# High and low parts of the projected rows in one tensor, and one 128-partition load for a query, a key's high part and compression rows

## The chip, the cores and the metric

One core of one Trainium2 chip runs the kernel. The metric is the device time of one execution in microseconds. Three runs of the kernel before gave 3173.43, 3173.92 and 3177.03 us, with a median of 3173.92 us.

## What is computed

One transformer layer over 2048 tokens of width 1024, in float32. Cut to what matters:

```python
h = rmsnorm(x, g_mix_pre)
z = h @ w_in                                   # queries, keys, values of all mixers, split by columns
o_a = nsa_mixer(...)                           # 6 heads: compressed + selected + window attention
o_b = dilated_mixer(...)                       # 3 pairs (window, dilation) x 4 heads
o_c = banded_attention(cq, ck, cv, 127, sinks) # 6 heads, window 128
x = x + rmsnorm(concatenate([o_a, o_b, o_c]) @ w_out, g_mix_post)
x = x + rmsnorm(conv_glu_ffn(rmsnorm(x, g_ffn_pre)), g_ffn_post)
```

The compression in `nsa_mixer` runs a small two-layer network over windows of 32 keys (and values), 16 apart.

## The kernel before

The program has four parts that follow one another, each a block in which the five engines run programs of their own with semaphores set by hand: `project` (to about 684 us), `compress` (to 723), `attend` (to about 1616) and `mix_ffn`. A block begins when all engines have left the one before.

Products in float32 are made of two roundings: a value is split in a high part (rounded) and a low part (the rest). `project` computes z transposed, one row of 2048 tokens for each of 33 x 128 columns of z, and stores the high parts in the DRAM tensor `z_hi` and the low ones in `z_lo` (lines 380 and 381). The rows that the compression needs go to `z_pair`, as (key or value, parity of the token, row, 1024 tokens).

`load_windows` (line 76) fetches compression rows for m = 0 (keys) and m = 1 (values): for each of two groups, the even tokens to partitions 0 to 63 and the odd ones to partitions 64 to 127, four loads of 256 KB for each m. SP issues them at the end of `project`'s program, with the 2 MB of first-layer weights (`load_first`, line 86) behind each m. In `compress` SP then loads the small weights, the queries of the first two attention units (lines 1227, 1228), two bias tables, and the first half of what the second key needs (`keys_in`, lines 1236, 1237). The block ends on SP with a wait for `units_in`, that is for the queries and the bias tables.

`attend` works through 36 units in a fixed order: six times a k unit (compressed keys) and two b units, then six c units, then six pairs of a w unit and an s unit. A unit has 16 steps, one for 128 tokens of queries. For a step PE makes scores with two products (lines 1907, 1908): the stationary operand is a query of 128 partitions, 64 rows of its high part over 64 rows of its low part; it meets `k_hi`, the key's high part twice (partitions 0 to 63 and 64 to 127), and `k_lo`, the low part over zeroes. So hi x hi, lo x hi and hi x lo are summed. DVE adds the bias and takes maxima (line 2108), ACT exponentiates (2022), PE turns the weights and multiplies them by values (1919, 1952). PE issues scores up to five steps ahead; its order is fixed, so a missing query or key holds up the turns and value products behind it, too.

A query and a key have two buffers each. A unit's query is two loads of 512 KB (`load_q`, lines 1681, 1682), a key three: the high part twice and the low part (`load_k`, lines 1693, 1694). SP issues them when the scores of the last unit that used the buffer are done (`sp.wait_ge(scored, through(u))`), then waits for `biased` and loads the bias table (`near`, line 1704), waits for `summed` and loads the values (line 1697), then waits for the output and stores it. The k units have no key load, since their keys stay on the chip. The three heads of a group share a key in the c, w and s units. PE waits for a query with its count of 32 for each turn of the buffer, and for a key with 48 (lines 1873 to 1879).

All of these transfers are issued on SP's hardware queue. There is one group of 16 DMA engines for the core, and a transfer's semaphore rises by 16 when all of it has landed.

Of the kernel before, what the change touches and what calls it, by code (L numbers as in the profile page):

```python
# [7 lines left out]
F32 = mybir.dt.float32  # L8
# [6 lines left out]
P = 128  # L15
T = 2048
# [59 lines left out]
def load_windows(eng, z_pair, x_raw, x_in, m):  # L76

    for g in range(2):
        for odd in range(2):
            eng.dma_start(x_raw[odd * HD:(odd + 1) * HD, m, g, :],  # L80
                          z_pair[m, odd, g * HD:(g + 1) * HD, :]).then_inc(x_in[m], 16)


def load_first(eng, w1_copy, w1_raw, w1_in, m):
# [1074 lines left out]


def compress(nc, z_pair, w1_copy, b1_t, w2, overlap, x_raw, w_raw, w_hi, poss, x_in, w_in, pos_in, last_out, keys_in, kc_hi, kc_lo, vk, idt,
             z_hi, z_lo, bias_b, cmp_bias, low, near):

    U = T // 2
    NW = NC + 3
# [1 line left out]
    with ExitStack() as ctx:  # L1167
# [48 lines left out]
        @blk.sync  # L1216
        def _(sp):
            load_first(sp, w1_copy, w_raw, w_in, 1)
            sp.dma_start(b1s[:], b1_t).then_inc(small_in, 16)
            for dup in range(2):  # L1220
                sp.dma_start(kw2[:, :, dup, :], w2[0].rearrange("(m p) n -> p m n", p=P)).then_inc(small_in, 16)
            sp.dma_start(vw2[:], w2[1].rearrange("(m p) n -> p m n", p=P)).then_inc(small_in, 16)

            first = attention_units()[:3]
            for s, unit in enumerate(first[:2]):
                rows = slice(unit.q_row, unit.q_row + HD)
                sp.dma_start(low[0:HD, s, :].bitcast(F32), z_hi[rows, :]).then_inc(units_in, 16)
                sp.dma_start(low[HD:P, s, :].bitcast(F32), z_lo[rows, :]).then_inc(units_in, 16)
            sp.dma_start(near[:, 0, 0:CW], cmp_bias[0]).then_inc(units_in, 16)
            sp.dma_start(near[:, 1, 0:2 * P], bias_b[0]).then_inc(units_in, 16)  # L1230
            rows = slice(first[2].k_row, first[2].k_row + HD)
            sp.wait_ge(zeroed, 3)
            for g in range(G):
                sp.dma_start(vk[:, g, HD + 1:], overlap).then_inc(over_in, 16)
            for half in range(2):
                sp.dma_start(low[half * HD:(half + 1) * HD, 2, :].bitcast(F32), z_hi[rows, :]).then_inc(keys_in, 16)
            sp.dma_start(low[0:HD, 3, :].bitcast(F32), z_lo[rows, :]).then_inc(keys_in, 16)
            sp.wait_ge(over_in, 16 * G)
            sp.wait_ge(last_out, 4 * 16)
            sp.wait_ge(units_in, 16 * 6)  # L1240

        @blk.gpsimd
        def _(pool):
# [55 lines left out]
        @blk.scalar  # L1299
        def _(act):  # L1300
            def upper(m):
                act.wait_ge(x_in[m], 64)
                for g in range(G):
                    act.activation(inside(x_hi, m, g), every_eighth(x_raw[:, m, g, :]), ACT.Copy).then_inc(xhi_done, 1)
                act.wait_ge(w_in[m], 16)
                for c in range(1 - m, 4):
                    act.activation(w_hi[:, m, quarter(c)], w_raw[:, m, quarter(c)], ACT.Copy).then_inc(whi_done, 1)

            act.wait_ge(pos_in, 32)
            for m in range(2):  # L1310
                for g in range(G):
                    act.activation(behind(x_hi, m, g), every_eighth(poss[:]), ACT.Copy).then_inc(poshi_done, 1)
            upper(0)
            upper(1)
            for m in range(2):
                for half in range(2):
                    act.wait_ge(hb_done, 2 * m + half + 1)
                    act.activation(h1[:, m, half, :].rearrange("p (g c) -> p g c", g=G),
                                   hid[:, 2 * m + half, 0:G * NW].rearrange("p (g c) -> p g c", g=G)[:, :, 0:NC],
                                   ACT.Gelu_apprx_tanh, bias=hb[:, m, half:half + 1]).then_inc(gelu_done, 1)  # L1320
            act.wait_ge(zeroed, 3)
            act.wait_ge(kc_done, 1)
            act.activation(kc_hi[:, :, 0:NC], kc_ps[:, 0:G * NC].rearrange("p (g c) -> p g c", g=G),
                           ACT.Copy).then_inc(khi_done, 1)
# [116 lines left out]
NARROW = 5 * P  # L1441


def attend(nc, idt, z_hi, z_lo, v_heads, gates, bias_b, bias_c, bias_s, bias_w, own_block, sinks, cmp_bias, pick_bias,
           kc_hi, kc_lo, vk, sel_t, parts, near_parts, o_heads, o_mid, q2, k_hi, k_lo, near, w_small, qm, vs,
           wo_copy, wo_moved, w_rows, w_in, first_o, o_last, keys_in):

# [122 lines left out]
    with ExitStack() as ctx:  # L1570
# [96 lines left out]
            v_count.append(v_seen[owner])  # L1667
        k_count, k_seen = [], [0, 0]
        for n, s in enumerate(kv_at.slot):
            k_seen[s] += 48 if n != 1 else 0  # L1670
            k_count.append(k_seen[s])
        out_count, out_seen = [], [0, 0]
        for n, s in enumerate(out_at.slot):
# [3 lines left out]
        @blk.sync  # L1677
        def _(sp):
            def load_q(n, u):
                rows, s = slice(units[u].q_row, units[u].q_row + HD), q_at.slot[n]  # L1680
                sp.dma_start(q2[0:HD, s, :].bitcast(F32), z_hi[rows, :]).then_inc(q_in[s], 16)
                sp.dma_start(q2[HD:P, s, :].bitcast(F32), z_lo[rows, :]).then_inc(q_in[s], 16)

            def load_qm(u):
                rows = slice(units[u].q_row, units[u].q_row + HD)
                sp.wait_ge(sel_out[units[u].h // R], 64)
                sp.dma_start(qm[0:HD, :].bitcast(F32), z_hi[rows, :]).then_inc(qm_in, 16)
                sp.dma_start(qm[HD:HD + NS, :].bitcast(F32), sel_t[units[u].h // R]).then_inc(qm_in, 16)

            def load_k(n, u):  # L1690
                rows, s = slice(units[u].k_row, units[u].k_row + HD), kv_at.slot[n]
                for half in range(2):
                    sp.dma_start(k_hi[s][half * HD:(half + 1) * HD, :].bitcast(F32), z_hi[rows, :]).then_inc(k_in[s], 16)
                sp.dma_start(k_lo[s][0:HD, :].bitcast(F32), z_lo[rows, :]).then_inc(k_in[s], 16)

            def load_v(n, u):
                sp.dma_start(vs[:, kv_at.slot[n]], v_heads[units[u].v_head]).then_inc(v_in[kv_at.slot[n]], 16)
# [168 lines left out]
        def _(pe):  # L1866
            def scores(n, only):
# [2 lines left out]
                ks = kv_at.slot[kv_at.of_unit[u]] if unit.kind != "k" else None  # L1870
                if t == 0 and only == 0:
                    if q_at.turn[q_at.of_unit[u]]:
                        pe.wait_ge(q_in[qs], 32 * q_at.turn[q_at.of_unit[u]])
                    if u == 1:
                        pe.wait_ge(zeroed, 1)
                    if unit.kind != "k" and kv_at.of_unit[u] == 1:
                        pe.wait_ge(keys_in, 48)
                    elif unit.kind != "k":
                        pe.wait_ge(k_in[ks], k_count[kv_at.of_unit[u]])
                    if unit.chosen:  # L1880
                        pe.wait_ge(qm_in, 32 * qm_at.of_unit[u] + 32)
                        pe.wait_ge(own_done, 1)
# [1349 lines left out]
def layer(nc, x, g_mix_pre, g_mix_post, g_ffn_pre, g_ffn_post, w_z, w_v, pos_t, w1, b1_t, w2, sinks, w_out, w_ffn,  # L3232
# [1 line left out]
    def scratch(name, shape, dt=F32):  # L3234
        return nc.dram_tensor(name, shape, dt, kind="Internal").ap()

    z_hi, z_lo = scratch("z_hi", [NZ * P, T]), scratch("z_lo", [NZ * P, T])
    v_heads, gates = scratch("v_heads", [2 * NV - 2, P, NT, HD + 1]), scratch("gates", [P, NT, 3 * NH_A])
    sel_t = scratch("sel_t", [G, NS, T])
    z_pair = scratch("z_pair", [2, 2, P, T // 2])  # L3240
# [6 lines left out]
    with ExitStack() as keep:  # L3247
# [13 lines left out]
        with ExitStack() as rows:  # L3261
            ops_f, ops = twin(nc, rows, "ops", [P, 10, T])
            poss = rows.enter_context(nc.sbuf_tensor("poss", [P, CMP // 2 + 8], F32))
            x_raw = ops[:, 2:4, :].bitcast(F32).rearrange("p m (g u) -> p m g u", g=G)
            w1_hi = ops[:, 0:8, :].rearrange("p (m a) (b n) -> p m a b n", m=2, n=HID)[:, :, 0:2].rearrange("p m a b n -> p m (a b) n")
            w1_raw = ops[:, 6:10, :].bitcast(F32).rearrange("p (m a) (b n) -> p m (a b) n", m=2, n=HID)
            project(nc, x, g_mix_pre, idt, ident, w_z, w_v, pos_t, z_hi, z_lo, z_pair, v_heads, gates, w1, w1_copy, w_out, wo_copy, wo_moved,
                    ops_f, ops, low, kc_f[:].rearrange("p a g n -> p (a g n)"), near[:].rearrange("p s n -> p (s n)"),
                    x_raw, w1_raw, poss, x2_in, w1_in, pos_in, last_out)
            compress(nc, z_pair, w1_copy, b1_t, w2, overlap, x_raw, w1_raw, w1_hi, poss, x2_in, w1_in, pos_in, last_out, keys_in,  # L3270
                     kc_hi, kc_lo, vk, idt, z_hi, z_lo, bias_b, cmp_bias, low, near)
        w_in = keep.enter_context(nc.semaphore("w_out_in"))
        k0_hi_f, k0_hi = twin(nc, keep, "k0_hi", [P, T])
        k0_lo_f, k0_lo = twin(nc, keep, "k0_lo", [P, T])
# [3 lines left out]
        with ExitStack() as mid:  # L3278
# [2 lines left out]
            first_o = low[:, 0, :].bitcast(F32).rearrange("p (k n) -> p k n", n=D)  # L3281
            narrow = w_small[:].rearrange("p s n -> p (s n)")
            w_rows += [narrow[:, a * D:(a + 1) * D] for a in range(3)] + [near[:].rearrange("p s n -> p (s n)")[:, 0:D]]
            attend(nc, idt, z_hi, z_lo, v_heads, gates, bias_b, bias_c, bias_s, bias_w, own_block, sinks, cmp_bias, pick,
                   kc_hi, kc_lo, vk, sel_t, parts, near_parts, o_heads, o_mid, low[:, 0:2, :],
                   (k0_hi[:], low[:, 2, :]), (k0_lo[:], low[:, 3, :]), near, w_small, qm, vs, wo_copy, wo_moved, w_rows, w_in, first_o, o_last, keys_in)
            mix_ffn(nc, idt, o_heads, o_mid, first_o, o_last, w_rows, w_in, x, g_mix_post, g_ffn_pre, g_ffn_post, x1, h2_rest, g_up,
# [61 lines left out]
```

## Time and profile before

| | |
|---|---|
| median of three runs | 3173.92 us |
| span of the profiled execution | 3174.1 us, of which PE is busy 3066.0 |
| granted clock of PE, mean | 0.991 of full speed |
| DMA, mean over the span | 134 GB/s |
| `project` | 0 to 684 us |
| `compress` | 684 to 723 us |
| k and b units, c units | 723 to 1104 us |
| w and s units | 1104 to 1616 us |

The page's first part gives the busy time of each engine. A view of stretches gives the same for a part of the span, with the granted clock and the mean busy share of the 16 DMA engines (which can come out slightly over 1) and what they moved. Issues of transfers are rows of SP's queue, and their time is that of the issue; "to landing" is the time from issue to the rise of the semaphore.

### The profile page before, as it was taken

Reading aid. Unit: us, or ns where it says so; the run is one execution under the profiler, and the core shown is the slowest. Engines: PE = TensorE matmul, PEld = TensorE weight load, DVE = VectorE, ACT = ScalarE, POOL = GpSimd, SP = SyncE. Lnnn points to the kernel's source line nnn. Section 1 sums busy time; section 2 is a strip of 40 time slices with the busy share of each in tenths; the row PEclk is TensorE's granted clock in tenths of the full one; section 3 lists DMA queues with packets and bytes.
Section 4 is the critical chain, followed back from the end, with each engine's and each line's share of the span. In section 5 each row is a group of like instructions: output and inputs, shape, how many; then the busy total and the mean of one; then the engine's idle time right before and its main releaser. Section 6 shows DMA issues by size and latency. Waiting matters only on the chain. (4 is left out here: it accounts for less than half of the span.)

```text
span 3174.1 us, 44910 instructions
## 1 busy us (share of the span) xinstructions
PE 3066.0 (97%) x16138; PEld 2501.5 (79%) x16138; DVE 2058.5 (65%) x3930; ACT 1472.0 (46%) x2657; POOL 1211.7 (38%) x845
## 2 busy tenths in 40 slices
PE   8999999998998999999989989999999999999998
PEld 8888888887776776666668878888888788888887
DVE  5565566556767987777744587777645577777443
ACT  5332533236666866665633444444434344444332
POOL 2444254310000024442110098888210698885010
PEclk9999999998999999999999999999999999999999
DMA  4465555378778743332234522222565222223553
GB/s 141 161 186 149 169 162 174 114 209 195 183 187 215 175 114 73 96 99 50 84 93 132 162 99 80 87 80 80 175 200 201 102 85 80 93 80 110 182 199 106
DMA packets 262540, 425.58 MB, mean 134 GB/s; under 512 B 126801, under 2 KB 162897, under 8 KB 250321
## 3 DMA queue, kind: packets, MB, share of 16 engines
q1 hardware_dynamic: 252752, 385.28, 41.4%
q0 software_dynamic: 9568, 37.43, 3.7%
q8 instruction: 131, 2.15, 0.3%
q14 instruction: 89, 0.72, 0.1%
HBM read 304.19 MB, written 126.84 MB: 136 GB/s over the span
## 5 line engine op out<-in xcount | busy, mean ns | idle before, releaser
L1080 PE MATMUL z_banks<-ops,z_area 128*128 128x512 f32 x1720 | 434.1, 391 | 3.2 <-DVE z_area L834 3.2
L3153 PE MATMUL f_banks<-f_wt 128*128 128x512 f32 x1776 | 406.1, 389 | 0.0
L3153 PEld LDWEIGHTS f_banks<-f_wt 128*128 128x128 f32 x1776 | 333.3, 188 | 69.2
L1080 PEld LDWEIGHTS z_banks<-ops,z_area 128*128 128x128 f32 x1720 | 323.0, 188 | 70.4 <-DVE z_area L834 3.6
L2540 POOL TENSOR_TENSOR f_wt<-f_wt_f,f_wt 128x1024 fp32r<-128x1024 f32 x132 | 320.2, 2449 | 60.3 <-ACT f_wt L2668 59.4
L2022 ACT ACTIVATE w_small<-w_small,a_stats 128x128 f32<-128x128 f32 (+3 forms) x510 | 257.3, 517 | 110.7 <-DVE a_stats L2108 82.6
L3124 PE MATMUL f_banks<-low,f_wt 128*128 128x512 f32 x704 | 275.3, 391 | 0.0
L2108 DVE CUSTOM_DVE_ANT_0 w_small<-a_s_ps,near 128x128 f32<-128x128 f32 (+2 forms) x456 | 166.2, 392 | 110.1 <-PE a_s_ps L1908 86.8
L2949 DVE SCALAR_TENSOR_TENSOR near<-w_small,vk,near 128x1024 f32<-128x1024 f32 x88 | 232.3, 2640 | 1.7
L3124 PE MATMUL f_banks<-f_oo,f_wt 128*128 128x512 f32 x704 | 218.0, 391 | 3.2 <-issue 3.0
L1952 PE MATMUL a_ot_ps<-a_turned_w,vs 128*64 128x256 f32 (+3 forms) x1452 | 220.9, 427 | 0.0
L1919 PE MATMUL a_t_ps<-idt,w_small 128*128 128x128 f32 x1092 | 214.7, 283 | 5.1 <-DVE a_turned_w L2011 2.6
L2011 ACT ACTIVATE a_turned_w<-a_t_ps 128x512 f32<-128x512 f32 (+3 forms) x255 | 137.2, 545 | 150.5 <-PE a_t_ps L1919 150.4
L2949 DVE SCALAR_TENSOR_TENSOR w_small<-w_small,vk 128x1024 f32<-128x1024 f32 x88 | 158.7, 1803 | 62.3 <-ACT w_small L2728 62.3
L2960 DVE TENSOR_TENSOR f_wt<-f_wt_f,f_wt 128x512 fp32r<-128x512 f32 x88 | 60.8, 690 | 205.6 <-ACT f_wt L2741 205.3
L3089 PE MATMUL f_banks<-f_wt,f_oo 128*128 128x512 f32 x768 | 179.3, 392 | 1.4 <-DVE f_wt L2503 1.4
L1952 PEld LDWEIGHTS a_ot_ps<-a_turned_w,vs 128*64 128x64 f32 x1452 | 105.9, 136 | 93.4 <-issue 76.0
L2733 ACT ACTIVATE near<-near 128x1024 f32<-128x1024 f32 x44 | 46.7, 1062 | 267.1 <-DVE near L2949 267.1
L1080 PE MATMUL z_banks<-low,z_area 128*128 128x512 f32 x560 | 168.3, 390 | 2.1 <-DVE z_st_lo L892 2.0
L2011 DVE COPY a_turned_w<-a_t_ps 128x512 f32<-128x512 f32 (+3 forms) x255 | 158.8, 624 | 17.5 <-PE a_t_ps L1919 15.6
L2738 ACT ACTIVATE f_wt<-f_wt_f 128x1024 fp32r<-128x1024 f32 x74 | 78.3, 1058 | 194.7 <-DMA f_wt_f<-in_w_ffn 194.6
L3089 PEld LDWEIGHTS f_banks<-f_wt,f_oo 128*128 128x128 f32 x768 | 142.7, 188 | 31.6 <-DVE f_wt L2503 2.7
(305 smaller groups left out, 7120.4 us busy)
## 6 DMA issues: line engine op xcount, KB each, us to landing
f_wt_f<-in_w_ffn SPq DMA_DIRECT2D x74, 512.0 KB, 4.1
z_area_f<-in_w_z SPq DMA_DIRECT2D x54, 512.0 KB, 5.1
low<-z_hi SPq DMA_DIRECT2D x48, 512.0 KB, 7.9
f_raw_f<-in_w_ffn SPq DMA_DIRECT2D x22, 1024.0 KB, 4.8
f_wt_f<-in_w_ffn SPq DMA_DIRECT2D x22, 1024.0 KB, 5.3
g_up<-near SPq DMA_DIRECT2D x44, 512.0 KB, 2.6
f_wt_f<-g_up SPq DMA_DIRECT2D x88, 256.0 KB, 4.4
low<-z_lo SPq DMA_DIRECT2D x39, 512.0 KB, 8.6
```

The source lines that it names most:

```text
L1080: last = pe.matmul(banks[:, bank, :], w[:, c * P:(c + 1) * P], rows[:, c * 512:(c + 1) * 512], start=(first and c == 0 and q == 0), stop=( ...
L1919: ins = pe.transpose(t_ps[:, b % TB, i, :], weights(n)[:, x * P:(x + 1) * P], idt[:])
L1952: ins = pe.matmul(ot_ps[lines, at:at + count * P], values, rows, start=(x == mine[0]), stop=(x == mine[-1]), skip_group_check=True)
L2011: ins = eng.activation(out, src, ACT.Copy) if e == 0 else eng.tensor_copy(out, src)
L2022: act.activation(weights(n), weights(n), ACT.Exp, bias=negm[:, n % 32:n % 32 + 1], scale=-1.0, accum_out=total).then_inc(weighed, 1)
L2108: dve.tensor_tensor_reduce(weights(n)[:, a:z], s_ps[:, c % SB, 0:z - a], table[:, at + a:at + z], -0.125, floor, ALU.add, ALU.min, low).th ...
L2540: pool.tensor_tensor(a_lo(n, first, count), src, a_hi(n, first, count).bitcast(F32), ALU.subtract)\
L2738: act.activation(hi, raw, ACT.Copy).then_inc(wdh_done, 1)
L2949: dve.scalar_tensor_tensor(out=acc[b], in0=u[:, b, i:HALF + i], scalar=cw[:, b, i, j:j + 1], in1=acc[b], op0=ALU.mult, op1=ALU.add).then_i ...
L3089: last = pe.matmul(mix[:, k, n * 512:(n + 1) * 512], oo[:, k, part, c, :], w_part(w, c)[:, n, :], start=(c == 0 and i == 0), stop=(c == DC ...
L3124: last = pe.matmul(banks[:, 4 * (n % 2) + bank, :], w[:, c * P:(c + 1) * P], rows[:, c * 512:(c + 1) * 512], start=(first and c == 0 and x ...
L3153: last = pe.matmul(banks[:, 2 * t + n, :], g[:, tok], w[:, n, :], start=(d == 0 and x == 0), stop=(d == NF - 1 and x == 2))
```

## The change

`z_hi` and `z_lo` become two halves of one DRAM tensor `z_parts` of shape (2, 33 x 128, 2048); `project` writes them as before. A unit's query is fetched by one load whose source is (2 parts, 64 rows, 2048), and a key's high part by one load whose source is the same 64 rows with a step of 0 over a leading count of 2. Compression rows come with source (2 parities, 64 rows, 1024). The destination of each has 128 partitions. The low part of a key stays a load of 64 partitions. The counts in the waits follow. Nothing is moved in the order of any engine.

```diff
 def load_windows(eng, z_pair, x_raw, x_in, m):
 
     for g in range(2):
-        for odd in range(2):
-            eng.dma_start(x_raw[odd * HD:(odd + 1) * HD, m, g, :],
-                          z_pair[m, odd, g * HD:(g + 1) * HD, :]).then_inc(x_in[m], 16)
+        eng.dma_start(x_raw[:, m, g, :], z_pair[m, :, g * HD:(g + 1) * HD, :]).then_inc(x_in[m], 16)
+
+
+def both_parts(z_parts, row):
+
+    return z_parts[:, row:row + HD, :]
+
+
+def upper_twice(z_parts, row):
+
+    return z_parts[0, row:row + HD, :].unsqueeze(0).to_broadcast([2, HD, T])
...
             for s, unit in enumerate(first[:2]):
-                rows = slice(unit.q_row, unit.q_row + HD)
-                sp.dma_start(low[0:HD, s, :].bitcast(F32), z_hi[rows, :]).then_inc(units_in, 16)
-                sp.dma_start(low[HD:P, s, :].bitcast(F32), z_lo[rows, :]).then_inc(units_in, 16)
+                sp.dma_start(low[:, s, :].bitcast(F32), both_parts(z_parts, unit.q_row)).then_inc(units_in, 16)
...
-            for half in range(2):
-                sp.dma_start(low[half * HD:(half + 1) * HD, 2, :].bitcast(F32), z_hi[rows, :]).then_inc(keys_in, 16)
-            sp.dma_start(low[0:HD, 3, :].bitcast(F32), z_lo[rows, :]).then_inc(keys_in, 16)
+            sp.dma_start(low[:, 2, :].bitcast(F32), upper_twice(z_parts, first[2].k_row)).then_inc(keys_in, 16)
+            sp.dma_start(low[0:HD, 3, :].bitcast(F32), z_parts[1, rows, :]).then_inc(keys_in, 16)
...
-            sp.wait_ge(units_in, 16 * 6)
+            sp.wait_ge(units_in, 16 * 4)
...
-                act.wait_ge(x_in[m], 64)
+                act.wait_ge(x_in[m], 32)
...
-            k_seen[s] += 48 if n != 1 else 0
+            k_seen[s] += 32 if n != 1 else 0
...
             def load_q(n, u):
-                rows, s = slice(units[u].q_row, units[u].q_row + HD), q_at.slot[n]
-                sp.dma_start(q2[0:HD, s, :].bitcast(F32), z_hi[rows, :]).then_inc(q_in[s], 16)
-                sp.dma_start(q2[HD:P, s, :].bitcast(F32), z_lo[rows, :]).then_inc(q_in[s], 16)
+                s = q_at.slot[n]
+                sp.dma_start(q2[:, s, :].bitcast(F32), both_parts(z_parts, units[u].q_row)).then_inc(q_in[s], 16)
 
             def load_qm(u):
                 rows = slice(units[u].q_row, units[u].q_row + HD)
                 sp.wait_ge(sel_out[units[u].h // R], 64)
-                sp.dma_start(qm[0:HD, :].bitcast(F32), z_hi[rows, :]).then_inc(qm_in, 16)
+                sp.dma_start(qm[0:HD, :].bitcast(F32), z_parts[0, rows, :]).then_inc(qm_in, 16)
                 sp.dma_start(qm[HD:HD + NS, :].bitcast(F32), sel_t[units[u].h // R]).then_inc(qm_in, 16)
 
             def load_k(n, u):
                 rows, s = slice(units[u].k_row, units[u].k_row + HD), kv_at.slot[n]
-                for half in range(2):
-                    sp.dma_start(k_hi[s][half * HD:(half + 1) * HD, :].bitcast(F32), z_hi[rows, :]).then_inc(k_in[s], 16)
-                sp.dma_start(k_lo[s][0:HD, :].bitcast(F32), z_lo[rows, :]).then_inc(k_in[s], 16)
+                sp.dma_start(k_hi[s].bitcast(F32), upper_twice(z_parts, units[u].k_row)).then_inc(k_in[s], 16)
+                sp.dma_start(k_lo[s][0:HD, :].bitcast(F32), z_parts[1, rows, :]).then_inc(k_in[s], 16)
...
-                        pe.wait_ge(q_in[qs], 32 * q_at.turn[q_at.of_unit[u]])
+                        pe.wait_ge(q_in[qs], 16 * q_at.turn[q_at.of_unit[u]])
...
-                        pe.wait_ge(keys_in, 48)
+                        pe.wait_ge(keys_in, 32)
...
-    z_hi, z_lo = scratch("z_hi", [NZ * P, T]), scratch("z_lo", [NZ * P, T])
+    z_parts = scratch("z_parts", [2, NZ * P, T])
+    z_hi, z_lo = z_parts[0], z_parts[1]
```

## Rows read from the trace of the kernel before

**Rows 1.** Busy time of the engines, from the page's first part

```profile
PE 3066.0 (97%) x16138; PEld 2501.5 (79%) x16138; DVE 2058.5 (65%) x3930; ACT 1472.0 (46%) x2657; POOL 1211.7 (38%) x845
```

**Rows 2.** Stretches: start:end, length, busy by engine, PE clock, DMA share, GB/s

```profile
675.00:723.00 48.00, 41.39 (x303) 38.30 (x301) 21.92 (x24) 20.44 (x25) 6.11 (x8) 1.00 1.05 248
...
723.00:739.00 16.00, 13.77 (x54) 11.01 (x54) 8.38 (x40) 8.36 (x20) 1.75 (x1) 0.51 0.74 181
...
723.00:1129.00 406.00, 372.75 (x2764) 300.10 (x2765) 307.09 (x1367) 285.58 (x915) 10.14 (x15) 0.96 0.81 193
...
1129.00:1600.00 471.00, 452.14 (x2908) 323.59 (x2907) 355.74 (x1250) 289.29 (x585) 151.09 (x199) 1.00 0.31 79
```

**Rows 3.** PE's waits: line, releaser, us in total, times, longest

```profile
PE a_s_ps L1907 <- DVE a_stats L2108: 19.5, 27, 2.3
```

**Rows 4.** Line 2108, 700 to 1110 us: what ended its engine's idle time

```profile
  DMA near<-in_bias_b: 9.1, 4
...
  DMA near<-in_cmp_bias: 1.5, 1
```

**Rows 5.** Timeline of PE: start, us, line, operation

```profile
720.62 1.10 PE L1295 MATMUL c_vc_ps<-c_vw,c_h 128*127 128x64 f32 x8
...
1103.21 0.30 PE L1907 MATMUL a_s_ps<-k_hi,low 128*128 128x128 f32 x1
```

**Rows 6.** Timeline of SP's queue around the compression

```profile
675.23 2.42 SPq L80 DMA_DIRECT2D ops<-z_pair  x4
...
678.33 6.79 SPq L80 DMA_DIRECT2D ops<-z_pair  x4
...
689.07 9.85 SPq L1219 DMA_DIRECT2D c_b1s<-in_b_t  x1
...
722.94 0.33 SPq L1724 DMA_DIRECT2D a_sink<-in_sinks  x1
```

**Rows 7.** Timeline of SP's queue in attend: query issues

```profile
738.98 0.45 SPq L1681 DMA_DIRECT2D low<-z_hi  x1
...
1014.08 0.45 SPq L1681 DMA_DIRECT2D low<-z_hi  x1
...
1173.49 0.48 SPq L1681 DMA_DIRECT2D low<-z_hi  x1
...
1256.71 0.48 SPq L1681 DMA_DIRECT2D low<-z_hi  x1
```

**Rows 8.** DMA issues: count, KB each, median us to landing

```profile
ops<-w_copy SPq DMA_DIRECT2D x2, 2048.0 KB, 14.8
...
near<-in_g_mix_pre SPq DMA_DIRECT2D x1, 512.0 KB, 4.8
```

**Rows 9.** Stretches of 10 us with quick transfers

```profile
1560.00:1570.00 10.00, 9.88 (x63) 7.22 (x62) 9.36 (x36) 7.93 (x15) 1.38 (x2) 1.00 0.87 347
2940.00:2950.00 10.00, 10.00 (x46) 8.28 (x45) 4.34 (x5) 1.69 (x2) 0.00 (x0) 1.00 0.98 374
3160.00:3170.00 10.00, 5.45 (x25) 4.17 (x23) 4.93 (x4) 2.23 (x4) 1.48 (x4) 1.00 0.26 105
```

**Rows 10.** SP's queue: packets, MB, share of 16 engines

```profile
q1 hardware_dynamic: 252752, 385.28, 41.4%
```

**Rows 11.** Line 1681, a query's high half: count, durations, landing

```profile
L1681 SPq DMA_DIRECT2D low<-z_hi x28: 448/451/3147, 739.0 to 1423.2; - x28
...
DMA to landing us min/median/max: 4.6/6.0/11.0
```

**Rows 12.** Line 1693, a key's high halves

```profile
L1693 SPq DMA_DIRECT2D k_hi<-z_hi x18: 450/597/1282, 723.8 to 1297.2; - x18
L1693 SPq DMA_DIRECT2D low<-z_hi x16: 596/597/675, 767.6 to 1342.1; - x16
...
DMA to landing us min/median/max: 6.5/10.3/15.6
```

**Rows 13.** Line 1908: score products of the s units, first to last

```profile
L1908 PE MATMUL a_s_ps<-low,qm x240: 273/394/405, 1129.4 to 1588.6; 96*128 96x512 f32 x96, 96*128 96x128 f32 x12, 96*128 96x384 f32 x12
```

More of the change, by code:

```diff
@@ L1161, in compress @@
 def compress(nc, z_pair, w1_copy, b1_t, w2, overlap, x_raw, w_raw, w_hi, poss, x_in, w_in, pos_in, last_out, keys_in, kc_hi, kc_lo, vk, idt,
-             z_hi, z_lo, bias_b, cmp_bias, low, near):
+             z_parts, bias_b, cmp_bias, low, near):
     U = T // 2
@@ L1441, with attend @@
 NARROW = 5 * P
-def attend(nc, idt, z_hi, z_lo, v_heads, gates, bias_b, bias_c, bias_s, bias_w, own_block, sinks, cmp_bias, pick_bias,
+def attend(nc, idt, z_parts, v_heads, gates, bias_b, bias_c, bias_s, bias_w, own_block, sinks, cmp_bias, pick_bias,
            kc_hi, kc_lo, vk, sel_t, parts, near_parts, o_heads, o_mid, q2, k_hi, k_lo, near, w_small, qm, vs,
@@ L3270, in layer @@
             compress(nc, z_pair, w1_copy, b1_t, w2, overlap, x_raw, w1_raw, w1_hi, poss, x2_in, w1_in, pos_in, last_out, keys_in,
-                     kc_hi, kc_lo, vk, idt, z_hi, z_lo, bias_b, cmp_bias, low, near)
+                     kc_hi, kc_lo, vk, idt, z_parts, bias_b, cmp_bias, low, near)
         w_in = keep.enter_context(nc.semaphore("w_out_in"))
@@ L3283, in layer @@
             w_rows += [narrow[:, a * D:(a + 1) * D] for a in range(3)] + [near[:].rearrange("p s n -> p (s n)")[:, 0:D]]
-            attend(nc, idt, z_hi, z_lo, v_heads, gates, bias_b, bias_c, bias_s, bias_w, own_block, sinks, cmp_bias, pick,
+            attend(nc, idt, z_parts, v_heads, gates, bias_b, bias_c, bias_s, bias_w, own_block, sinks, cmp_bias, pick,
                    kc_hi, kc_lo, vk, sel_t, parts, near_parts, o_heads, o_mid, low[:, 0:2, :],
```

## The prediction

> **What bounds the kernel now.** I read the page's busy table first: PE works 3066.0 of 3174.1 us, so a removed wait can bring 108 us at most, while a new one is paid in full [rows 1]. Then the stretches: the change touches loads between 675 and 1600 us, the compression (675 to 723), the eighteen k and b units and six c units (723 to 1129, with the first w unit) and the s stage (1129 to 1600). PE is idle there for 6.6, 33.3 and 18.9 us; the 16 DMA engines are busy at 1.05, 0.81 and 0.31 [rows 2]. So in the first two stretches the transfers stand close behind the arithmetic. Next the waits: none of PE's is put down to a DMA, the largest is for DVE's bias step with 19.5 us [rows 3], and that step in turn waited for the bias tile five times, 9.1 + 1.5 us [rows 4]. PE's last product of the compression ends at 721.7 and SP issues attend's first transfer at 722.9 [rows 5, 6]: the unit loads at the compression's end are in by then. Loads of queries and keys come just in time now, and nothing more than that.
>
> **What goes.** 28 query pairs in attend and 2 in compress become one issue each, 18 key pairs too, and 8 window loads become 4. That spares SP about 0.6 us an issue (four window issues took 2.42 us [rows 6]); per b unit 1.2 us, by which the near load behind them is issued earlier. Bytes are the same: a pair of 512 KB loads becomes one of 1 MB. The waits change in count only (32 to 16, 48 to 32, 64 to 32), so no engine waits for another event than before; what is queued behind a late one is all of PE's program, since the scores of a unit stand in its order ahead of turns and value products of earlier units, and SP's next `scored` wait behind those. Price of this part alone: between 0 and the 10.7 us that DVE waited for near [rows 4].
>
> **What comes: a source with a leading count of 2.** A source was a block of rows, 64 or 128 deep; now it is (2 parts, 64 rows, 2048 columns), for the key with a step of 0 over the 2. Every transfer of before has a row count of 32 or more outermost on both sides, the replicated gain row included: 128 copies with a zero step, 512 KB in 4.8 us [rows 8], so the zero step by itself is harmless. No row shows what a leading 2 does. The ends: still 16 engines, or as many as the outer level has pieces, two. If transfers are dealt to engines by cutting the outermost level (one start and one step for each engine, which fits all transfers shown), only two engines move each of these loads while 14 look on. I take two, as the cut that needs nothing but the outer level, and keep 16 as a rival.
>
> The Trainium skill, page "DMA: Bandwidth & Descriptors", sections "Why a DMA increments its semaphore by 16 and not by 1" and "Rules for kernel authors", says this cut is the chip's: the engine count is the largest number up to 16 that divides the outermost counts of both patterns, and a leading broadcast of c copies confines a DMA to c engines, the lowest-numbered. Nothing in the trace of before tests it. By it all these loads also share the same two engines. Against it stands "SBUF — State Buffer", section "Door 1: The DMA port swizzle": 64 partitions reach half of the ports, 128 all, which speaks for the change; with this alone the sum would be the rival below.
>
> **Rate of one engine.** GB/s over 16 times the busy share: 347/(16 x 0.87) = 24.9, 374/(16 x 0.98) = 23.9, 105/(16 x 0.26) = 25.2 [rows 9]; over the whole queue 385.28 MB/(16 x 0.414 x 3174 us) = 18.3 [rows 10]; in the attention stretch 193/(16 x 0.81) = 14.9 [rows 2], but there 16 engines crowd on 64 partitions. Two engines alone crowd on nothing, so I take 25 GB/s; ends 27.5 (a tenth over the best row) and 18.3. A 1 MB load (1.049 MB, 0.524 MB an engine) takes 21.0 us instead of the 6 to 10 us in which its halves land now [rows 11, 12]. The Trainium skill, page "SBUF — State Buffer", section "Door 1: The DMA port swizzle", gives 27.2 GB/s for one port; by it the forecast would be some 3690 us.
>
> **The sum.** One of the two engines is a single line of work; I add its bytes.
> 1. From 675.2 us [rows 6] to the last unit load that the compression block waits for: windows 4 x 0.262 = 1.05 MB, its sixteenth of two 2 MB weight loads 0.26 MB [rows 8], queries 2 x 0.524 = 1.05 MB, small ones 0.03: 2.39 MB, at 25 GB/s 96 us, so 771, and 2 us to land, the bound from which attend can start. The compression itself (its windows land after 10 and 31 us, its second weights by about 730, PE then needs some 25 us) is done before that. Attend starts at 777 instead of 722.9: +54 us.
> 2. From there to the first s unit: 24 of 30 queries less the two already loaded = 22, and 16 of 18 keys, make 38 loads, 19.9 MB. Beside them a sixteenth of 16 low keys, 15 values, 22 outputs (all about 0.53 MB) and of bias tables: 2.0 MB. 21.9 MB at 25 GB/s are 878 us; 773 + 878 = 1651, against 1129.4 [rows 13]: +522 us. Does the engine ever rest? A unit's loads go out when the scores two units before are done, and a unit takes 16 us now (17 intervals between the query issues at 739.0 and 1014.1 [rows 7]). A triple k, b, b loads 5 MB of the new form: 5 x 21.0 + 10 us for the rest = 115 us, where PE needs 48, or at most 96 at the lower clock of 1.2 GHz, which it was granted (0.51) in a stretch with 14% idle time [rows 2]. The loads rule everywhere. The c units (21 us of load, some 15 of PE, up to 27 at half clock) may add 5 us each: +20 in all.
> 3. In the s stage (83 us a pair of w and s, 1173.5 to 1256.7 [rows 7]) a query load of 21 us is hidden beside an s unit; what it delays is the qm and far loads behind it, 27 us after the last scores, where PE reaches an s unit 26 us after its w unit began (1103.2 to 1129.4 [rows 5, 13]): 1 to 2 us for four pairs. Where the group changes, the key is in front too, 48 us against 26: +22. Together +28.
> 4. The mixer and the feed-forward part have none of these loads: 0.
> Sum: 3174.1 + 522 + 20 + 28 = 3744 (the 54 of step 1 are inside the 522), and 26 us allowed for what does not overlap, a landing or an issue at each of some twenty units where PE waits: 3770. The span is 3174.1 us and the median 3173.92, so nothing lies around it.
> At 18.3 GB/s steps 1 and 2 take 24.3/18.3 = 1328 us, end at 2005 and give 3174 + 876 + 70 = 4120, at 27.5 GB/s 884 us, 1561, and 3174 + 432 + 45 = 3650.
>
> **Rivals.**
> - All 16 engines take part. For it: the sixteen units of the semaphore are posted for every transfer, and the broadcast gain row. Then 128-partition loads may be quicker than 193 GB/s (347 and 374 in others [rows 9]), near lands sooner and DVE's 10.7 us go, with 2 to 4 us at the start of attend: 3160, between 3150 and 3180. This is the one that ends faster or unchanged; it decides if the load is cut at the level of rows.
> - Two engines, but each at its mean rate of 18.3 GB/s or less, since only two queues are fetched from and their packets share with all other loads: 4120. Against it: rates of 24 and more wherever long rows move without crowding.
> - Only the zero-step source is confined, since the two parts of a query might be lowered to rows: 16 keys then take 8.4 MB on an engine and everything else 3 MB, 456 us from 675 to 1131, hardly later than now on average, but a b unit then waits for 21 us of key and a burst of both: some 3 us for 18 units and 21 us at the start, 3250.
>
> **How the numbers follow.** Forecast 0.64, slow engines 0.18, sixteen engines 0.12, only the broadcast 0.06. The likeliest gives 3770. The range from 3640 to 4180 holds the first two with the bounds of the rate and leaves out 0.18. A measurement here tells 0.2% (6 us) from no change: slower holds 0.64 + 0.18 + 0.06 and 0.01 of the sixteen, 0.89; faster 0.08, same 0.03.
>
> **What would show it.** Right: 1 MB loads that land 21 us or more after issue, and the later of two after 40 or more; DMA share near 2/16 = 0.13 to 0.2 and 50 to 70 GB/s between 775 and 1650 us, where it was 0.81 and 193; waits of PE on query or key DMAs of 20 to 70 us a unit; a lower granted clock there; the first s scores near 1670 us, and the same 2045 us plus about 28 behind them. Wrong: landing in 6 to 10 us, which is the sixteen; query loads that land quickly beside slow keys, which is the third rival. If the stretch is as long as said but the engine count is another, or the loads wait for SP, whose issues stall when its queue is full (one took 9.85 us [rows 6]), the cause is not the one named here.

## The result, and the profile after

The changed kernel takes 3806.48 us (median of 3805.62 to 3807.58), against 3173.68 us for the kernel before on the same chip: a ratio of 1.1992, 95% interval 1.1975 to 1.2009. It is 633 us slower. The profiled execution spans 3805.8 us, where the one of before spanned 3174.1.

The page's first two parts of the changed kernel come first. The second part cuts the span into 40 slices of 95 us and gives busy tenths, the granted clock of PE in tenths, the DMA share in tenths and GB/s.

```profile
PE 3146.9 (83%) x16138; PEld 2567.9 (67%) x16138; DVE 2063.8 (54%) x3930; ACT 1475.9 (39%) x2657; POOL 1211.5 (32%) x845
...
PE   9999999533455434567988999999999999999999
...
PEclk9999999866767666788999999999999999999999
DMA  4455454322222223222342134522225632222553
GB/s 147 157 180 175 147 163 128 116 77 85 86 78 83 71 82 99 85 85 68 81 111 66 34 106 127 167 78 86 81 78 177 233 122 89 85 82 83 175 187 113
```

The program has 44858 instructions, 52 fewer than before: the 52 issues that were joined. The loss is in slices 8 to 19, from about 670 to 1810 us. There PE is busy three to five tenths (six and seven in the last two slices), the DMA engines are busy two or three tenths and move some 80 GB/s, where before PE worked 373 of 406 us and the DMA engines' share was 0.81 [rows 2]. PE's own busy time grew by 81 us only, for as many products at a lower clock. That PE rests and the transfers get thinner at the same time points to transfers that use few of the DMA engines. The stretches say the same (start:end, length, busy by engine, PE clock, DMA share, GB/s):

```profile
675.00:720.00 45.00, 11.00 (x61) 9.02 (x60) 2.08 (x3) 1.83 (x3) 0.00 (x0) 0.69 0.38 116
...
800.00:1600.00 800.00, 371.92 (x2295) 297.01 (x2295) 252.43 (x1142) 235.22 (x760) 7.40 (x12) 0.68 0.25 83
```

Next PE's waits in the changed kernel (releaser, us in total, times, longest), and the first and last score products of the s units:

```profile
PE a_s_ps L1910 <- DVE a_stats L2111: 261.1, 32, 22.2
PE a_s_ps L1910 <- DMA low<-z_parts: 163.8, 22, 13.5
PE a_s_ps L1910 <- issue: 97.2, 4, 30.3
PE c_vc_ps L73 <- PEq L138: 32.6, 1, 32.6
```

```profile
L1911 PE MATMUL a_s_ps<-low,qm x240: 273/394/522, 1735.5 to 2220.5; 96*128 96x512 f32 x96, 96*128 96x128 f32 x12, 96*128 96x384 f32 x12
```

The wait for DVE [rows 3] grew from 19.5 to 261.1 us, and waits for queries stand where there were none. The 32.6 us are PE's wait for the compression block, which it begins at 720 us instead of 684, since SP stalls on the second pair of windows for 25 us. The DVE waits are DMA waits at one remove: DVE itself waited for bias tables that stand behind queries and keys on the queue, as its line of the waits between 675 and 1760 us shows. [rows 4] had 9.1 and 1.5 us there.

```profile
DVE w_small L2111 <- DMA near<-in_bias_b: 166.8, 5, 34.4
...
DVE w_small L2111 <- DMA near<-in_cmp_bias: 141.7, 5, 31.4
```

SP's queue shows the pace. These are query and key issues (start, us of the issue itself) of the changed kernel; the four query rows given are the ones behind a b unit at the same place of four successive triples k, b, b. A triple takes 116.4, 122.2 and 117.0 us, where it took 48 [rows 7].

```profile
783.13 0.33 SPq L1727 DMA_DIRECT2D a_sink<-in_sinks  x1
...
842.85 7.74 SPq L1686 DMA_DIRECT2D low<-z_parts  x1
...
959.23 9.63 SPq L1686 DMA_DIRECT2D low<-z_parts  x1
...
1003.99 31.11 SPq L1697 DMA_DIRECT2D low<-z_parts  x1
...
1081.44 3.94 SPq L1686 DMA_DIRECT2D low<-z_parts  x1
...
1198.40 4.83 SPq L1686 DMA_DIRECT2D low<-z_parts  x1
```

The issues themselves now stall, up to 31 us for a key's low part (0.6 us before). We read this as SP being unable to hand over a transfer while the queue is full; no view shows how full the queue is.

### The profile page after: what moved, and what is told of

It reads as the page before. It is cut to its first block and busy times, and to the rows that moved or that the text cites. A ratio compares the mean times of both kernels' runs of the same rounds, so it can differ in the third digit from the quotient of the medians.

```text
span 3805.8 us, 44858 instructions
## 1 busy us (share of the span) xinstructions
PE 3146.9 (83%) x16138; PEld 2567.9 (67%) x16138; DVE 2063.8 (54%) x3930; ACT 1475.9 (39%) x2657; POOL 1211.5 (32%) x845
## 3 DMA queue, kind: packets, MB, share of 16 engines
q1 hardware_dynamic: 251192, 385.28, 31.4%
## 5 line engine op out<-in xcount | busy, mean ns | idle before, releaser
L2111 DVE CUSTOM_DVE_ANT_0 w_small<-a_s_ps,near 128x128 f32<-128x128 f32 (+2 forms) x456 | 166.9, 393 | 474.7 <-DMA near<-in_bias_b 166.8
L1910 PE MATMUL a_s_ps<-k_hi,low 128*128 128x256 f32 (+3 forms) x312 | 130.4, 421 | 257.6 <-DVE a_stats L2111 126.9
L2543 POOL TENSOR_TENSOR f_wt<-f_wt_f,f_wt 128x1024 fp32r<-128x1024 f32 x132 | 320.0, 2446 | 60.2 <-ACT f_wt L2671 59.3
L1910 PE MATMUL a_s_ps<-low 128*128 128x512 f32 (+3 forms) x384 | 167.8, 439 | 125.6 <-DMA low<-z_parts 54.3
L1910 PEld LDWEIGHTS a_s_ps<-k_hi,low 128*128 128x128 f32 x312 | 69.7, 223 | 285.8 <-DVE a_stats L2111 131.0
L1922 PE MATMUL a_t_ps<-idt,w_small 128*128 128x128 f32 x1092 | 234.8, 306 | 3.2 <-DVE a_turned_w L2014 1.9
L1955 PE MATMUL a_ot_ps<-a_turned_w,vs 128*64 128x256 f32 (+3 forms) x1452 | 233.9, 448 | 0.0
L1846 POOL TENSOR_TENSOR a_oh<-a_oh,a_add 128x256 f32<-128x256 f32 x48 | 32.9, 685 | 474.5 <-DVE a_add L2170 474.2
L1910 PEld LDWEIGHTS a_s_ps<-low 128*128 128x128 f32 x384 | 82.1, 214 | 139.9 <-issue 58.6
## 6 DMA issues: line engine op xcount, KB each, us to landing
low<-z_parts SPq DMA_DIRECT2D x39, 1024.0 KB
f_raw_f<-in_w_ffn SPq DMA_DIRECT2D x22, 1024.0 KB, 4.8
f_wt_f<-in_w_ffn SPq DMA_DIRECT2D x22, 1024.0 KB, 5.2
```

Source lines behind the costliest of these rows:

```text
L1910: pe.matmul(out, query, hi[:, start + a:start + z], start=True, stop=False)
L1922: ins = pe.transpose(t_ps[:, b % TB, i, :], weights(n)[:, x * P:(x + 1) * P], idt[:])
L1955: ins = pe.matmul(ot_ps[lines, at:at + count * P], values, rows, start=(x == mine[0]), stop=(x == mine[-1]), skip_group_check=True)
L2111: dve.tensor_tensor_reduce(weights(n)[:, a:z], s_ps[:, c % SB, 0:z - a], table[:, at + a:at + z], -0.125, floor, ALU.add, ALU.min, low).th ...
L2543: pool.tensor_tensor(a_lo(n, first, count), src, a_hi(n, first, count).bitcast(F32), ALU.subtract)\
```

## The experiments

The theory stated before them: a load whose source has a leading count of c is dealt to c DMA engines, so the changed loads share two, and the bytes on either of these set the time from 675 us to the first s unit. Here and below, the line is the work of one of these two engines, in megabytes, and c is the leading count of a source. Rivals: the new place of the rows in memory; the zero step or the size of 1 MB; SP's stalled issues; the order of the bias tables.

### One part undone at a time

Windows back (`e1_windows_back`):

```diff
-        eng.dma_start(x_raw[:, m, g, :], z_pair[m, :, g * HD:(g + 1) * HD, :]).then_inc(x_in[m], 16)
+        for odd in range(2):
+            eng.dma_start(x_raw[odd * HD:(odd + 1) * HD, m, g, :],
+                          z_pair[m, odd, g * HD:(g + 1) * HD, :]).then_inc(x_in[m], 16)
```

> The change with only the compression windows loaded as before, in eight loads of 64 partitions. Two-engine theory (each load with a leading source count of 2 runs on two of the 16 DMA engines, a line of work that sets the stage): 1.05 MB less on that line, at 22.9 GB/s 46 us less than the changed kernel, 3760 us. If SP's stalled issues rather than the engines set the time: the 25 us issue of the second pair of windows goes, and 3780 us. If all 16 engines serve these loads: no change, 3806 us.

Measured: 3773.1 us, 33 less than the changed kernel, between the 3760 of two engines and the 3780 of SP's stalled issues: this run alone doesn't tell the two apart. The expectation took off too much, too: windows spread over 16 engines still leave 0.13 MB on each, so 0.92 MB go, 37 to 40 us.

Queries back (`e2_queries_back`), in compress and in attend:

```diff
-                sp.dma_start(q2[:, s, :].bitcast(F32), both_parts(z_parts, units[u].q_row)).then_inc(q_in[s], 16)
+                for half in range(2):
+                    sp.dma_start(q2[half * HD:(half + 1) * HD, s, :].bitcast(F32),
+                                 z_parts[half, units[u].q_row:units[u].q_row + HD, :]).then_inc(q_in[s], 16)
```

> The change with only the queries loaded as before (two loads of 64 partitions), keys and windows as changed. Two-engine theory: of 40 loads of 0.524 MB on the line up to the first s unit 16 keys stay, and queries give a sixteenth each; windows 1.05, weights 0.26, keys 8.4, queries 24 x 0.066 = 1.6, other 2.0 MB: 13.3 MB at 22.9 GB/s are 581 us, from 675 to 1256 instead of 1129, so 3174 + 127 + some 30 where a key is awaited alone: 3330 us. If only queries were confined: 3174 us. If only keys: 3806 us.

Measured: 3496.7 us (ratio 1.1017, 1.0995 to 1.1039), 310 less than the changed kernel.

Keys back (`e3_keys_back`):

```diff
-                sp.dma_start(k_hi[s].bitcast(F32), upper_twice(z_parts, units[u].k_row)).then_inc(k_in[s], 16)
+                for half in range(2):
+                    sp.dma_start(k_hi[s][half * HD:(half + 1) * HD, :].bitcast(F32), z_parts[0, rows, :]).then_inc(k_in[s], 16)
```

> The change with only the keys' high parts loaded as before (two loads of 64 partitions), queries and windows as changed. Two-engine theory: 24 queries of 0.524 MB (12.6), keys 1.05, windows 1.05, weights 0.26, other 2.0 MB: 17.0 MB at 22.9 GB/s are 741 us, from 675 to 1416 instead of 1129: 3174 + 287 + 25 = 3490 us. If only the zero-step source were confined: 3180 us. The three parts undone one by one should nearly add up to the whole loss in the order windows < keys < queries.

Measured: 3572.9 us (1.1257, 1.1234 to 1.1279), 233 less.

All three back, the one tensor kept (`e4_one_tensor`, the three diffs above together):

> Only the tensor change is left: z_parts with both halves in one DRAM tensor, all loads of 64 partitions as in the kernel before. Two-engine theory: 3174 us, ratio 1.000 within 0.002. If the new addresses of the rows (other HBM placement) are part of the loss: more than 3180 us.

Measured: 3175.1 us, ratio 1.0004 (0.9995 to 1.0014).

So the tensor costs nothing and the three forms of load cost everything. Queries and keys each carry a large part, so it isn't the zero step of the key alone; the two parts of a query, with no zero step, are as bad. Both kernels with one of them undone are slower than the bytes gave, by 167 and 83 us. With the queries back, a triple took some 85 us for 1.5 MB on an engine: 17 to 18 GB/s, or the line rested. That is taken up below.

### The leading count varied

The same 128 destination partitions, the same bytes and length of row, the same waits; the source is 128/c rows, broadcast c times (`e_copies_4`, `e_copies_8`, `e_copies_16`). The values that arrive are not those of the layer. For c = 4, the windows likewise:

```diff
-    return z_parts[:, row:row + HD, :]
+    return z_parts[0, row:row + 32, :].unsqueeze(0).to_broadcast([4, 32, T])
...
-    return z_parts[0, row:row + HD, :].unsqueeze(0).to_broadcast([2, HD, T])
+    return z_parts[0, row:row + 32, :].unsqueeze(0).to_broadcast([4, 32, T])
```

> Queries, keys' high parts and windows each as one 128-partition load of the same size, but the source is 32 rows with a leading broadcast count of 4 (the values that arrive are wrong for the layer; the destination, the bytes, the runs and every wait are those of the changed kernel). If a load runs on as many engines as the leading count (theory): 0.262 MB an engine, 11 us a load; line from 675 to the first s unit 2.0 + 0.26 + 0.5 + 40 x 0.262 = 13.3 MB, 580 us at 22.9 GB/s: about 3330 us, with the bias tables held up behind the keys up to 3400. If the engine count is always two: 3806. If all 16 whatever the count: the changed kernel would have been fast, which it is not.

> As before with a leading count of 8 (16 rows broadcast 8 times). Theory: 8 engines, 0.131 MB each, 5.7 us a load, no longer more than PE needs for a unit: 3170 to 3230 us. If the loss came from the broadcast itself or from 128-partition loads of 1 MB on SP's queue: above 3700 us.

> As before with a leading count of 16 (8 rows broadcast 16 times). Theory: all 16 engines with 0.066 MB each, and SP issues one load for two: equal to the kernel before or up to 20 us faster, 3155 to 3180 us. If the loss came from 1 MB loads with a step of 0, above 3700 us. It is also the price of the change with all engines at work.

Measured: 3456.3, 3340.4 and 3175.2 us, the last with a ratio of 1.0000 (0.9991 to 1.0010). The leading count takes the time from 3806 (c = 2) to 3175 (c = 16). With 4 and 8 both expectations were missed: 3456 us is 56 above the 3400 that allowed for late bias tables, and 3340 is 110 above the upper end of 3230. So c engines at the same 23 GB/s each is not the whole account; this is taken up below. The number of distinct rows read falls along with c, too, from 64 or 128 to 8; that it isn't the cause is argued, not tested: the kernel before reads 64 distinct rows a load and is as fast as c = 16. With 16 the same 1 MB loads land again, by the issues of that kernel (KB each, median us from issue to landing; the same row of the changed kernel's page ends at 1024.0 KB, without a landing), and the first s product is back at 1128.0 us:

```profile
low<-z_parts SPq DMA_DIRECT2D x39, 1024.0 KB, 9.1
```

```profile
L1911 PE MATMUL a_s_ps<-low,qm x240: 274/393/406, 1128.0 to 1587.2; 96*128 96x512 f32 x96, 96*128 96x128 f32 x12, 96*128 96x384 f32 x12
```

That rules out the broadcast, the size of the load and the 128 partitions. The mechanism fits the Trainium skill, page "DMA: Bandwidth & Descriptors", section "Rules for kernel authors": a small outermost count c confines a transfer to at most c engines. That the engines are c in number is still an inference here, since no view names the engine of a transfer; that the time hangs on c is shown. The busy share of the 16 engines fits it: between 800 and 1100 us it is 0.25, 0.41 and 0.63 for c = 2, 4 and 8, which is c/16 and 0.13 to 0.16 more for all other loads. The run with c = 16 also measures what the change would have brought with all engines at work: nothing.

### Bytes, or issues and descriptors

`e_half_columns` moves half of each row in attend:

```diff
-                sp.dma_start(q2[:, s, :].bitcast(F32), both_parts(z_parts, units[u].q_row)).then_inc(q_in[s], 16)
+                sp.dma_start(q2[:, s, 0:T // 2].bitcast(F32), both_parts(z_parts, units[u].q_row)[:, :, 0:T // 2]).then_inc(q_in[s], 16)
...
-                sp.dma_start(k_hi[s].bitcast(F32), upper_twice(z_parts, units[u].k_row)).then_inc(k_in[s], 16)
+                z = T // 2 if n else T
+                sp.dma_start(k_hi[s][:, 0:z].bitcast(F32), upper_twice(z_parts, units[u].k_row)[:, :, 0:z]).then_inc(k_in[s], 16)
```

> The changed kernel, with only the first 1024 of 2048 columns of each query and key high part loaded in attend (the first key of its buffer whole): the rest of the buffer keeps older rows, so scores are not those of the layer, while the number of rows, loads and waits stays. Line of 25.4 MB at 23.9 GB/s (the changed kernel, 675 to 1735 us) less 37 x 0.262 = 9.7 MB: 15.7 MB, 657 us, to 1332: 3174 + 203 + 25 = 3400 us if bytes on two engines set the time. If the number of descriptors or SP's issues did: above 3700 us.

Measured: 3441.2 us (1.0835, 1.0815 to 1.0855). Half of the bytes, with as many rows and issues, took away 365 of 633 us. The packets on SP's queue are 251192 in both kernels. So bytes set most of the time and not the number of issues, rows or packets; that SP's stalls follow from a queue that is drained slowly fits this. The 41 us over the expectation stay open, and grow a little with the right count: 38 loads are halved up to the first s product, not 37, which leaves 15.4 MB.

### The place of the bias tables

```diff
                 sp.wait_ge(scored, through(u))
+                sp.wait_ge(biased, through(u))
+                for n, x in near_at.after.get(u, []):
+                    load_near(n, x)
                 for n, x in q_at.after.get(u, []):
                     load_q(n, x)
...
-                sp.wait_ge(biased, through(u))
-                for n, x in near_at.after.get(u, []):
-                    load_near(n, x)
```

It was put into the changed kernel (`e_near_first`), the one with the queries back, the one with c = 8, and the kernel before.

> The changed kernel with each unit's bias table issued ahead of its query and key loads instead of behind them (SP waits for biased first, some us later than for scored). If the line of work on two engines alone sets the time, with the bias table's place in it indifferent: 3806 us, within 15. If PE waits in turn for a bias table behind a key that is needed only a unit later, so that the line rests between (DVE waited 370 us for bias tables in the changed kernel): 60 to 120 us less, about 3720 us.

Measured: 3815.4 us, 9 more than the changed kernel. Here DVE waits for no bias table, where it waited 166.8 + 141.7 us and more in the changed kernel; PE's waits for DVE fall from 261.1 to 23.5 us, and its waits for queries rise from 163.8 to 429.1 us:

```profile
PE a_s_ps L1911 <- DMA low<-z_parts: 429.1, 22, 37.0
```

The line on two engines is full, and which of its transfers comes first is nearly indifferent. A wait that is large in the profile was not what set the time.

> Queries as before, keys and windows on a leading count of 2, and each unit's bias table issued ahead of its query and key. With the queries back the kernel took 3497 us, where the bytes of the two-engine line give 3330: a triple of units took 84 to 88 us for 1.5 MB an engine, 61 us at 24.6 GB/s. Order theory: there the line rests, since a bias table stands behind a key needed later and lands 30 us after its issue; moved ahead, 80 to 150 us less, 3350 to 3410 us. Rate theory: the two engines are slower when 64-partition loads share them, and the order is indifferent: 3480 to 3510 us.

Measured: 3440.3 us, 57 less than with the queries back alone. That lies between the two theories: the order is a part of that kernel's excess of 167 us, and 110 us stay. DVE's waits for bias tables are gone from its list, and PE waits 146 us for queries instead.

> The loads with a leading broadcast count of 8 (wrong values for the layer, same bytes), with the bias table issued first. That kernel took 3340 us although 8 engines have only 5.7 us of work at 23 GB/s for a load. Order theory: bias tables behind keys, so 60 to 130 us less, 3210 to 3280 us. Rate theory: each of the eight engines moves 8 to 13 GB/s only (a query, a key and a low key, 0.3 MB an engine, were followed by a bias table that landed 27 us after issue), the line is full and the order is indifferent: 3320 to 3350 us.

Measured: 3318.1 us, 22 less. The order is a small part there; what is left fits the slower rate of each engine, for which this run is no separate proof.

> The kernel before with each unit's bias table issued ahead of its query and key, nothing else. DVE waited 10.7 us in total for bias tables that stood behind 2.5 MB of other loads. If those waits are on the path: 3163 to 3168 us, ratio 0.997 to 0.998. If the queries land later by what the bias tables land earlier, or SP's wait for biased delays the loads: 3174 to 3180 us, ratio 1.000 to 1.002.

Measured: 3163.2 us, ratio 0.9958 (0.9945 to 0.9972), 0.42% faster than the kernel before and faster than everything else here. DVE's waits for bias tables are gone between 700 and 1110 us; they land 4.6 us after issue (11.6 before), while queries land as before (5.7 us, 6.0 before [rows 11]). In that kernel the issues read:

```profile
L1704 SPq DMA_DIRECT2D near<-in_bias_b x11: 332/333/333, 738.8 to 970.4; - x11
...
DMA to landing us min/median/max: 1.8/4.6/9.7
```

```profile
L1909 PE MATMUL a_s_ps<-low,qm x240: 273/393/406, 1118.4 to 1577.6; 96*128 96x512 f32 x96, 96*128 96x128 f32 x12, 96*128 96x384 f32 x12
```

The first s product comes at 1118.4 instead of 1129.4 us [rows 13], 11 us earlier, as much as the whole gain and as much as DVE's 10.7 us of waits [rows 4]. But the gain isn't these waits alone. Up to its first s product, PE has this stretch from 723 us on:

```profile
723.00:1118.00 395.00, 366.88 (x2764) 295.73 (x2765) 306.97 (x1367) 285.14 (x915) 10.20 (x15) 0.98 0.82 198
```

Against the 406 us of [rows 2] with the same 2764 products, 5.1 us are idle time of PE (28.1 instead of 33.3), and 5.9 are busy time (366.9 instead of 372.8), at a granted clock of 0.98 instead of 0.96 of full speed.

## Why the prediction was right, point by point

The forecast was 3770 us in a range from 3640 to 4180; 3806 was measured. It rested on two engines for each of the new loads, a choice for which no row of before spoke, as the prediction says; the runs with other leading counts showed that the time hangs on that count. The closeness of the number is in part luck, since its errors offset each other in part: 42 us for two loads left out and 22 us more of rate, against 26 us allowed without a row.

**Step 1, to the start of attend: +54 us forecast, +60.2 measured** (783.1 against 722.9 [rows 6]). The compression was expected to be done before the block's last unit load, and was: PE ended it at 755.7 us, and SP waited 4.5 us more for the last bias table. The windows did not land after 10 and 31 us, as the prediction has it. A pair is 0.52 MB on an engine, so its own rate gives 21 us, and 47 for the second; the second was in at 731 us. Nothing hung on this.

**Step 2, to the first s unit: the term that was mis-sized.** Forecast, with its 20 us of rest, about 1670 us; measured 1735.5. The larger cause is a count. The prediction took two preloaded queries off 24; but 24 is what SP issues in attend up to there, 28 issues less the four of later s-stage heads, with the two preloaded on top. So 40 loads stand on the line, not 38: 42 us at 21.0 us each. The rest is rate. With the right count the line holds 25.4 MB from 675 to 1735.5 us, 23.9 GB/s against 25; by one triple it is 5 x 0.524 + 0.26 = 2.88 MB in 117 us, 24.6 GB/s. Here the nearest rows [rows 9] gave the rate to 5%; the forecast of 115 us a triple came within 7.2 us for each of the three shown. The rest of 5 us in each c unit is there: from the query issue at 1517.0 to that at 1684.6 us five queries and one key went out, 3.1 + 0.4 = 3.5 MB, which take 142 us at 24.6 GB/s, in 168 us.

```profile
1517.04 5.84 SPq L1686 DMA_DIRECT2D low<-z_parts  x1
...
1684.57 0.53 SPq L1686 DMA_DIRECT2D low<-z_parts  x1
```

So the shift of the first s product, 606.1 us (1735.5 - 1129.4 [rows 13]), is 42 us for the two loads, 542 us as forecast (522 + 20) and 22 us more.

**Step 3, the s stage: +28 us forecast, +25.6 measured**: 3805.8 - 1735.5 = 2070.3 us, against 3174.1 - 1129.4 = 2044.7.

**Step 4: nothing in the rest**, as the slices show from 1800 us on.

**The allowance of 26 us** for landings and issues that do not overlap rested on no row. The 22 us over in step 2 took nearly all of it; whether as such or as a rate of 24.6 instead of 25 GB/s (25.4 MB take 17 us longer) can't be told. With the two loads counted, the forecast would have been 3812 us.

**The rivals.** Sixteen engines: fallen, by the changed kernel's time and the runs with c = 4 to 16. Its own price, 3160 us, was wrong too: with c = 16 the kernel takes 3175.2, since a bias table behind a 1 MB load lands no earlier (12.8 us in that kernel, 11.6 before). The gain that the prediction put on DVE's 10.7 us exists, but comes from the order of the loads, not from their number. Slow engines at 18.3 GB/s: fallen for c = 2. Only the zero-step source: fallen by the queries, which cost more than the keys. The rule that the prediction cites from the Trainium skill, page "SBUF — State Buffer", section "Door 1: The DMA port swizzle", that 128 partitions reach all ports and 64 half of them, brought nothing here with c = 16: a query of 1 MB lands 8.0 us after its issue in the median, and before its second half landed 7.5 us after an issue that came 0.5 us later.

**The signs.** PE's waits (30.3 us at the longest, forecast 20 to 70 a unit) and the lower clock (0.68) came as said, the first s product 65 us late. The landing of the 1 MB loads can't be read, since the changed kernel's page gives none; the bias tables behind them land 29.5 us after issue in the median, 11.6 before. The DMA share and rate did not come as said: 0.25 and 83 GB/s from 775 to 1650 us, forecast 0.13 to 0.2 and 50 to 70. The bytes up to the first s product are the same 90 MB as before ([rows 2]: 248 GB/s for 48 us and 193 for 406), which over the forecast's own 976 us are 92 GB/s; that sign was worked out wrong, and the sum does not use it.

**What the prediction did not see** is how the parts combine. Undone singly they return 33, 310 and 233 us, 576 of 633, but each kernel with one large part left is slower than its bytes at 22.9 GB/s. The line's average up to the first s product falls as it gets shorter: 25.4 MB in 1060 us for the change, 23.9 GB/s; 18.0 MB in 841 with the keys back, 21.4; 15.4 MB in 717 with half columns, 21.5; 13.4 MB in 768 with the queries back, 17.5, and 19.0 with the bias tables first; 13.8 MB in 724 for c = 4, 19.1; 8.06 MB in 592 for c = 8 with the bias tables first, 13.6. A part of that is rest, as the order of the bias tables showed. How much of the remainder is rest and how much a slower engine was not separated. For c = 8 the busy share speaks for slower engines: 141 GB/s at a share of 0.63 (800 to 1100 us) are 14.0 GB/s for a busy engine, all loads taken together, where c = 2 gives 82/(16 x 0.25) = 20.5 and the kernel before 14.9 [rows 2].

## What to carry to other kernels

Before two transfers are joined to one, read the outermost level of both access patterns: a destination of 128 partitions doesn't help when the source begins with a count of 2. A joined load saves its issue only, so ask first who waits for that issue; here nobody did, while the small table that the next engine needs first stood last in the same queue, and moving it ahead gave 0.42%. And where a line of work is full, the wait that the profile names largest may only be its shadow: ask whether the order matters by changing it.

## What the runs showed of the hardware beyond the forecast

- Behind loads of 1 MB with c = 2 the issues on SP's queue stall: up to the s stage, a key's low part took 17.4 us (`k_lo`) and 19.9 us (`low`) to issue in the median and 31.1 at the most, against 0.6 before and with c = 16. Transfers behind it in SP's program, with more rows outermost, wait for that.
- Going from c = 2 to c = 8 does not make the line four times as quick. If c is the number of engines, two carried 2 x 23.9 = 48 GB/s up to the first s product and eight 8 x 13.6 = 109 (rests included, an estimate from the sums above). With c = 8 a bias table issued behind a query, a key and a low key (0.3 MB an engine, by the same reading) landed 26.7 us after issue in the median between 780 and 1100 us, and the kernel lost 165 us; with c = 16 it lost nothing. What slows the eight was not tried.
- PE's granted clock went from 0.96 to 0.68 of 2.4 GHz in the mean of the stage while PE was busy less than half of the time, and its busy time rose by 81 us for the same number of products. Of that, 74 us lie between 675 us and the first s product (489.1 us for 3072 products, against 414.5 for 3070), in the shadow of the loads.
